# Two block sums of the first chunk pair moved further back in VectorE's order

## What is computed

```python
D_MODEL, SEQ, DEPTH, D_FF = 1024, 256, 2, 2816
def swiglu(h, w_gate, w_up, w_down):
    return (jax.nn.silu(h @ w_gate) * (h @ w_up)) @ w_down
...
x = x + 0.5 * swiglu(rmsnorm(x, norm_g[layer, 0]), ffn_w_gate[layer, 0], ffn_w_up[layer, 0], ffn_w_down[layer, 0])
x = x + hybrid_mixer(...)
x = x + 0.5 * swiglu(rmsnorm(x, norm_g[layer, 2]), ffn_w_gate[layer, 1], ffn_w_up[layer, 1], ffn_w_down[layer, 1])
```

## Time and profile before

| | us |
|---|---|
| median of 3 runs | 2618.75 (2618.14 to 2620.67) |
| the profiled execution's own time | 2618.59 |
| its span in the profile | 2616.8 |
| TensorE busy | 2584.4 |
| VectorE busy | 1801.2 |
| ScalarE busy | 1554.9 |
| GpSimd busy | 849.9 |

### The profile page before, as it was taken

The page is one execution under the profiler, slowest core; times in us unless marked ns, Lnnn a source line. Parts: engine busy times, 40 slices in busy tenths (PEclk is TensorE's granted clock), DMA queues, the critical chain, the costliest instruction groups (busy, mean ns, idle before and its releaser), DMA issues.

```text
span 2616.8 us, 42862 instructions
## 1 busy us (share of the span) xinstructions
PE 2584.4 (99%) x16554; PEld 2239.9 (86%) x16554; DVE 1801.2 (69%) x2641; ACT 1554.9 (59%) x2202; POOL 849.9 (32%) x443
## 2 busy tenths in 40 slices
PE   9999999999999999999999999999999999999999
PEld 7888998888888998888889999988878899999787
DVE  6873645876863745876876787368768767873686
ACT  5655665656565655656565745665655657456655
POOL 0007672000017675000008754810100187548100
PEclk9999999999999999999999999999999999999999
DMA  9546548547545548548548732585485387425752
GB/s 287 178 132 178 145 152 252 172 152 242 182 131 176 145 161 252 181 136 251 180 111 191 172 83 82 175 252 180 134 257 178 98 202 161 86 78 186 241 185 97
DMA packets 349931, 447.20 MB, mean 171 GB/s; under 512 B 30398, under 2 KB 239296, under 8 KB 349728
## 3 DMA queue, kind: packets, MB, share of 16 engines
q1 hardware_dynamic: 347984, 442.80, 56.8%
q10 hardware_dynamic: 816, 1.21, 0.1%
q0 software_dynamic: 928, 0.45, 0.1%
HBM read 443.31 MB, written 1.05 MB: 170 GB/s over the span
## 4 chain that ended last, share of the span: by engine, by line
PE 88%; ACT 4%; SPq 3%; DVE 2%; DMA 2%; issue 1%; DVEq 0%; ACTq 0%
PE PS L610 27%; PE PS L612 26%; PE PS L611 26%; SPq L403 1%; PE PS L863 1%; ACT wp L634 1%; DMA ring<-in_ffn_w_up_dram 1%; PE PS L1284 1%; DMA ring<-in_ffn_w_in_dram 1%; PE PS L1357 1%; DVE wp L642 1%; ACT xh L1494 1%; SPq L431 1%; PE PS L1347 1%; PE PS L1087 1%
## 5 line engine op out<-in xcount | busy, mean ns | idle before, releaser
L642 POOL TENSOR_TENSOR wp<-ring,wp 128x1024 fp32r<-128x1024 f32 (+2 forms) x332 | 786.0, 2385 | 1480.1 <-ACT wp L634 1479.7
L634 ACT ACTIVATE wp<-ring 128x1024 fp32r<-128x1024 f32 x712 | 746.7, 1054 | 558.5 <-PE PS L610 370.0
L642 DVE TENSOR_TENSOR wp<-ring,wp 128x1024 fp32r<-128x1024 f32 x380 | 459.4, 1221 | 198.5 <-ACT wp L634 198.1
L610 PE MATMUL PS<-wp,xh 128*128 128x512 f32 (+2 forms) x1440 | 567.2, 394 | 3.9 <-DVE wp L642 2.3
L612 PE MATMUL PS<-wp,xl 128*128 128x512 f32 (+2 forms) x1440 | 557.7, 387 | 0.0
L611 PE MATMUL PS<-wp,xh 128*128 128x512 f32 (+2 forms) x1312 | 506.9, 386 | 0.0
L610 PE MATMUL PS<-xh,wp 128*128 128x256 f32 x1536 | 444.8, 290 | 0.1
L612 PE MATMUL PS<-xh,wp 128*128 128x256 f32 x1536 | 434.4, 283 | 0.0
L611 PE MATMUL PS<-xl,wp 128*128 128x256 f32 x1536 | 434.3, 283 | 0.0
L610 PE MATMUL PS<-wp,hh 128*128 128x512 f32 x832 | 329.1, 396 | 5.9 <-ACT W L1623 5.9
L610 PEld LDWEIGHTS PS<-wp,xh 128*128 128x128 f32 x1440 | 270.5, 188 | 68.3 <-issue 8.9
(11 more groups left out here) (354 smaller groups left out, 3526.3 us busy)
## 6 DMA issues: line engine op xcount, KB each, us to landing
ring<-in_mix_w_in_dram SPq DMA_DIRECT2D x256, 256.0 KB, 3.8
ring<-in_ffn_w_in_dram SPq DMA_DIRECT2D x224, 256.0 KB, 3.6
ring<-in_ffn_w_down_dram SPq DMA_DIRECT2D x176, 256.0 KB, 3.6
ring<-in_w_in_dram SPq DMA_DIRECT2D x176, 256.0 KB, 3.0
ring<-in_ffn_w_out_dram SPq DMA_DIRECT2D x176, 256.0 KB, 3.8
W<-in_ffn_w_in_dram SPq DMA_DIRECT2D x64, 512.0 KB, 7.0
ring<-in_ffn_w_gate_dram SPq DMA_DIRECT2D x112, 256.0 KB, 3.2
ring<-in_ffn_w_up_dram SPq DMA_DIRECT2D x112, 256.0 KB, 4.0
```

The source lines that it names most:

```text
L610: first_ = mm(o, w[0], x[0], start=start, stop=False, skip_group_check=True)
L634: act_(dst, src, ACT.Copy).then_inc(hi_ready, 1)
L642: (engine or v_).tensor_tensor(dst, src, part_views(t, wh)[0], ALU.subtract).then_inc(lo[t.slot()], 1)
```

## The change

In the first pair of every FFN (`p == 0`), `block3` and `block4` no longer stand ahead of `two_chunks`. `block3` comes after the two halves of M6's low part, `block4` after the low part of M7. No instruction is added or taken away, and only VectorE's order differs.

```diff
@@ -2348,9 +2348,12 @@
                 low_behind("M6", 0)
                 low_behind("M6", 1)
                 if p == 0:
+                    block3(p)
                     gated(c - 1)
                 low_whole(p, "M3", "T3")
                 low_whole(p, "M7", "T3")
+                if p == 0:
+                    block4(p)
                 low_behind("M2", 0)
                 low_behind("M2", 1)
                 if p == 0:
@@ -2390,8 +2393,6 @@
             low_whole(0, "M1", "T1")
             turned(PLAIN - 2)
             low_whole(0, "M5", "T2")
-            block3(0)
-            block4(0)
             two_chunks(0, *PAIRS[0])
```

## The result

| | before | changed |
|---|---|---|
| median, us (19 runs of each) | 2617.48 | 2623.43 |
| lowest to highest, us | 2616.74 to 2620.67 | 2621.04 to 2626.52 |
| ratio, 95% interval | | 1.0021 [1.0014, 1.0028] |
| span of the profiled execution, us | 2616.8 | 2623.0 |

A forecast was written before the change was run, and what follows sets the result against it. The prediction took VectorE's queue from M5's low part to `c22` to set M4's start. New waits of 1.07 and 0.17 us less 0.52 gave 0.72 us, eight times 5.8, on 2618.75: 2624.5 us, range 2621.5 to 2627.5.

The forecast's parts named there:

- M4 starts when VectorE is done with c22: First pair of each FFN: VectorE's queue from M5's low part to `c22` sets M4's start; forecast 0.72 us later.
- TensorE may run early or late in between: Between M5 and M4 in the first pair, TensorE's timing does not matter; VectorE's waits count.
- M6's own wait: M6 starts 0.90 us late, waiting for its low part on VectorE; after the change it follows M5 at once.
- The releaser that the trace named: Rival: M6 really waits for `m5s`, stays at 98.22 and delays M4 by 1.5 us; 2630.8 us, 3 in 100.
- VectorE's waits: Idling for M1's slot (1.07 us) and M7's high part (0.17) comes in; 0.52 ahead of M4's low part goes.
- The sum: M4 0.72 us later in each of eight FFNs, 5.8 us in all, forecast 2624.5 us, 0.22% slower.
- Nothing swallows it behind the pair: Everything behind M4 shifts together; the rival, a later wait swallowing the 0.72 us, gave 2618.75 us, 3 in 100.
- The clock: Rival: two close stalls lower TensorE's clock during M4, 2.7 us in each FFN, 2646 us; 2 in 100.
- The rule on VectorE's flush: Rival: VectorE serialises fully, about 0.6 us more in each FFN up to `c22`, 2629.5 us; 1 in 100.
- The rivals: Six other outcomes, at 2606, 2614.6, 2618.75, 2630.8, 2629.5 and 2646 us, with 1 to 4 in 100 each.
- M7's low part at 99.3: Condition of the rival that VectorE meets no new wait: M4 0.5 us earlier, 2614.6 us; 4 in 100.
- The side of 0.2%: Whether the whole kernel's change passes 0.2% (5.2 us): slower 0.64, within 0.33, faster 0.03.

## Why the prediction was right

- *M4 starts when VectorE is done with c22.* Right in the changed kernel, where `c22` ends 0.10 us ahead of M4, and in five of the six experiments; in the changed kernel with `c12` put behind, TensorE itself was the bound, held by M2, with `c22` done 0.15 us ahead of M4. Four orders of VectorE gave 13.8, 13.8, 13.1 and 12.0 us as worked out from its queue, and in the kernel before with `c12` put behind, ScalarE's high part of M4 held VectorE as expected. Too broad is the sentence that TensorE may run early or late in between: in the kernel before, VectorE's 0.44 us of idle time hang on the turn behind M3. In the changed kernel this makes no difference: VectorE comes to M4's low part 10.81 us after M5's last matmul (108.93 - 98.12), and even in the kernel before M4's high part let it start at 10.08 (107.17 - 97.09). With both sums ahead it does: M4's low part starts at 9.01 there (105.43 - 96.42) without a wait, which a turn as late as in the kernel before would not have let it do.
- *M6's own wait.* Right: M6's low part ends early and M6 starts 0.22 us after M5's last matmul, with `m5s` no earlier than before. The releaser that the trace named, ScalarE's line 1623, was not the one.
- *VectorE's waits.* 1.07 and 0.17 us were to come in by spacings, 0.52 to go. The rows show 0.99 and 0.18 of idle time; the first is counted from the end of M5's low part, 0.08 behind the earliest next start, so it is the same 1.07. The second pair of the same trace had both waits to read the earlier trace rows. Added up, the two look like two costs, of which the first is the larger; the run with t4 alone moved shows that they are not. There the first is gone and the loss is the same 0.72 us, because M7's low part still starts 2.94 us after M5's last matmul. What makes the loss is that start, which the prediction has from the earlier trace rows, and t4 behind it.
- *The sum.* 0.72 us in each FFN, measured 0.71 to 0.74; 5.8 us in all, measured 5.95 by the medians. Ahead of M2 about 0.8 us and ahead of M4 about 1 us were forecast; the idle times are 0.70 and 0.97.
- *Nothing swallows it behind the pair.* Right: the time follows eight times the distance to 1 us in the changed kernel and in four of the six experiments; in the two with `c12` put behind it does so to 1 us once the late down tile is counted (3.6 us expected that way against 3.7 in the kernel before so edited, 0.1 against 1.0 in the changed one).
- *The clock.* It did not fall: the mean granted clock of the profiled execution is 1.0, the 2.4 GHz level, with the two waits in each pair.
- *The rule on VectorE's flush* (the Trainium skill, "VectorE: DVE Perf Modes", "Terms") would have given 2629.5, if it is read as adding up the rows' full durations. The rows after the change again overlap, t3 from 95.68 for 2.29 with the next start at 97.88, and the time agrees with the spacings.
- *The rivals.* One condition is misread: M7's low part at 99.3 would leave M4 where it was in the kernel before (100.02 - 0.72); for M4 0.5 us earlier it had to start by about 98.8. It started 2.93 us after M5's last matmul, which is 100.02 in the prediction's times, so nothing hangs on it.
- *The side of 0.2%.* That the ratio came out above 0.2% is in part luck: the interval, 1.0014 to 1.0028, has room on both sides of it.
- The predicted 2624.5 stood on a median of 2618.75 for the kernel before, whose median over more runs is 2617.48; the measured 2623.43 is lower by about that much.

## What to carry to other kernels

A wait of the busiest engine is worth its length only if that engine is not held again by the same queue a few steps on: look for the last wait of the stage, find whose queue ends there, and count that queue's own idle times. A reordering that only changes what that queue does first gains what idle time it fills and loses what new waits it meets; put work into gaps that exist (ahead of a part that is not yet wanted), rather than behind the part that is wanted next. Where the same sequence runs elsewhere in the program in the new order, as in the second pair here, its rows give the new waits beforehand.

## What the runs showed that was not expected

Putting `c12` behind `c22` cost 0.44 to 0.45 us per FFN at the first tile of the down projection, through ScalarE's order: a sum that M4 does not need releases an activation, behind which the next weights' high part stands in the queue. And the gain of both sums put ahead, 9.5 us, is a little over the 8.7 us that the pair's distance explains; the difference, 0.8 us, is smaller than the spread of the runs (2607.50 to 2609.51), and whether anything is behind it is open.
